# Moving TensorE's branch hint in two mixture-of-experts loops from the head of a pass to a point ahead of its last down projections

## The chip, the cores and the metric

The kernel runs on one core of one Trainium2 chip. The metric is the device time of one execution in microseconds (us), taken as the median of several runs.

## The reference

Two transformer blocks one after the other, batch 1, 256 tokens, width 1024, all in float32. The first block is attention beside a state-space mixer, then a mixture of experts with 16 experts (512 hidden units each, two per token). The second block is three kinds of attention, merged by gates, then a mixture of experts with 32 experts (1024 hidden units each, four per token). What matters here are the two mixtures, cut to their core:

```
for e in range(MOE_EXPERTS):                      # first block, 16 experts
    he = jax.nn.silu(h @ w_gate[e]) * (h @ w_up[e])
    out = out + combine[..., e:e + 1] * (he @ w_down[e])

def expert_block(rows, e):                        # second block, 32 experts
    hb = xt[rows] @ w1[e] + b1[e]
    g, u = clip(hb[:, :D_EXPERT]), clip(hb[:, D_EXPERT:])
    glu = g * jax.nn.sigmoid(g * SWIGLU_ALPHA)
    return ((u + 1.0) * glu) @ w2[e] + b2[e]
```

## The kernel before

Each engine has its own hand-written instruction stream: SyncE (SP) issues the weight loads, TensorE (PE) multiplies, ScalarE (ACT) and VectorE (DVE) do what lies between. They meet at semaphores alone.

**Weights** stream from HBM through a ring of six slots in SBUF (`ring`), 2 MB a load. SP issues the load of a slot when PE has counted the product that read it last (`PD`, "products_done"). An expert of the first mixture reads three slots (gate, up, down), one of the second six (gate and up of the first 512 hidden units, gate and up of the other 512, two down halves).

**The tokens of an expert** are gathered by a matmul with a 0/1 matrix (`gather`, L1676), so an expert multiplies only with the tokens that chose it. Their number comes in three sizes: up to 64, up to 128, and all 256 tokens. `size_of` loads the size of an expert from SBUF into a register, and `by_size` (L376) writes a body once for each size, each inside an `If` on that register. So the compiled program holds three bodies at each such place and runs one. With up to 64 tokens the two halves of the columns run on different halves of the array.

**An expert on PE** (`expert`, L1721) issues in this order:

- `half_up` (L1605, matmuls at L1621, the bias of the second mixture at L1626): the gate half into PSUM pair 0, then the up half into pair 1. The second mixture does both twice.
- between them `scatter` (L1682, matmuls at L1694): the finished rows of the expert before go back to their tokens.
- `turn_hidden` (L1632, L1639): transposes of the hidden rows. In the second mixture it stands twice, and the second one waits for the second half of the hidden units.
- `gather` (L1666, L1676): the rows of the next expert.
- a wait for `outputs_added`, then `half_down` (L1644; L1657 for up to 64 tokens, L1660 for more): one down half in the first mixture, two in the second.
- `turn_picks` (L1700; L1707 for up to 64 tokens, L1709 for more): transposes of the 0/1 matrix.

**The loops.** `experts(b, j0, n)` (L1714) runs mixture `b` with `n` experts. After a first `gather` it opens a loop over pairs of experts: `looped(pe, 0, n // 2)` (L1767) gives 8 passes for the first mixture and 16 for the second, and each pass holds two experts (`par` 0 and 1).
**What sets the order** around the change is the order of calls in `expert` alone. The first loop is called at L1774, between `ranks` (L1598) and the transposes of the residual (`transposes("p0", ...)`, L1777). The second is called at L1881 and is PE's last work.

Of the kernel before, what the change touches and what calls it, by code (L numbers as in the profile page):

```python
# [29 lines left out]
def build(nc, a):  # L30
# [11 lines left out]
    with ctx:  # L42
        sems = {}

        def sem(name):
            if name not in sems:
                sems[name] = ctx.enter_context(nc.semaphore(name))
            return sems[name]
# [247 lines left out]
        def uses_before(j):  # L296

            return 16 * (j // RING + 1)
# [69 lines left out]
        def size_of(eng, e):  # L368

            return eng.value_load(sizes[0:1, bass.ds(e + 1, 1)], min_val=0, max_val=2)  # L370

        def looped(eng, start, end):  # L372

            return nc.Fori(start, end, engines=[eng.engine], hint_back_edge=True)

        def by_size(eng, size, body):  # L376

            for c, w in enumerate((H2, P, T)):
                with eng.If(size == c):
                    body(w)  # L380
# [995 lines left out]
        def _(pe):  # L1376
# [255 lines left out]
            def turn_hidden(b, half, size):  # L1632

                o = ps[2 - b]
                src = HID[:, half]

                def body(w):
                    for c in range(4 * w // P):
                        ins = nc.tensor.transpose(o[:, P * c:P * c + P], src[:, P * c:P * c + P], ident)  # L1639
                    ins.then_inc(sem(f"hidden_turned{b}"), 1)  # L1640

                by_size(pe, size, body)
# [39 lines left out]
            def scatter(b, e, size):  # L1682

                pe.wait_ge(sem(f"ys_ready{b}"), e + 1)

                def body(w):
                    if w == T:
                        pe.drain().then_inc(sem(f"scattered{b}"), 1)
                        return
                    for t in range(NT):  # L1690
                        for h in range(2):
                            r = slice(H2 * h, H2 * h + H2) if w == H2 else slice(0, P)
                            y = YS[r, 0:512] if w == H2 else YS[:, 512 * h:512 * h + 512]
                            ins = mm(ps[2 + t][:, 512 * h:512 * h + 512], pickT[r, P * t:P * t + P], y, start=True,  # L1694
                                     stop=True)
                    ins.then_inc(sem(f"scattered{b}"), 1)

                by_size(pe, size, body)

            def turn_picks(b, buf, size):  # L1700

                def body(w):
                    for t in range(NT):
                        o = ps[1][:, P * t:P * t + P]
                        if w == H2:
                            for h in range(2):
                                ins = mm(o[H2 * h:H2 * h + H2, :], pick[:, buf, t, 0:H2], ident, start=True, stop=True)  # L1707
                        else:
                            ins = nc.tensor.transpose(o, pick[:, buf, t], ident)  # L1709
                    ins.then_inc(sem(f"pick_turned{b}"), 1)  # L1710

                by_size(pe, size, body)

            def experts(b, j0, n):  # L1714

                nh = b
                nk = 3 * nh
                hidden = sem(f"hidden_ready{b}")
                hiddenT = sem(f"hiddenT_ready{b}")

                def expert(i, par, size, size_before, size_next):  # L1721
                    e = 2 * i + par
                    j = j0 + nk * par

                    def value(jj):
                        return 16 * (2 * nk // RING) * i + uses_before(jj)

                    if b == 2:
                        pe.wait_ge(sem(f"b1_loaded{par}"), 16 * i + 16)
                    for half in range(nh):  # L1730
                        if half:
                            pe.wait_ge(sem("gate_limited"), 2 * e + 1)
                        else:
                            pe.wait_ge(sem(f"xg_ready{b}"), e + 1)
                        half_up(j, value(j), ps[0], size, (half, par) if b == 2 else None)
                        if half:
                            pe.wait_ge(up_free, 2 * e + 1)
                        else:
                            pe.wait_ge(sem(f"pickT_ready{b}"), e + 1)
                        half_up(j + 1, value(j + 1), ps[1], size, (2 + half, par) if b == 2 else None)  # L1740
                        j += 2
                        if half == 0:
                            scatter(b, e, size_before)
                    if b == 1:
                        pe.wait_ge(hidden, e + 1)
                        turn_hidden(b, 0, size)
                        gather(b, e + 1, 1 - par, size_next)
                    else:
                        pe.wait_ge(hidden, 2 * e + 1)
                        pe.wait_ge(sem("gate_limited"), 2 * e + 2)  # L1750
                        turn_hidden(b, 0, size)
                        pe.wait_ge(up_free, 2 * e + 2)
                        gather(b, e + 1, 1 - par, size_next)
                        pe.wait_ge(hidden, 2 * e + 2)
                        pe.wait_ge(hiddenT, 2 * e + 1)
                        turn_hidden(b, 1, size)
                    pe.wait_ge(sem(f"outputs_added{b}"), e + 1)
                    for half in range(nh):
                        pe.wait_ge(hiddenT, nh * e + (half + 1))
                        half_down(j, value(j), HIDT[:, half], size, half == 0, half == nh - 1)  # L1760
                        j += 1
                    if b == 2:
                        pe.wait_ge(sem(f"xg_ready{b}"), e + 2)
                    turn_picks(b, par, size)

                gather(b, 0, 0, size_of(pe, 0))
                with looped(pe, 0, n // 2) as i:  # L1767
                    for par in range(2):
                        e = 2 * i + par
                        expert(i, par, size_of(pe, e), size_of(pe, e - 1), size_of(pe, e + 1))  # L1770
                pe.wait_ge(sem(f"pickT_ready{b}"), n + 1)
                scatter(b, n, size_of(pe, n - 1))  # L1772

            experts(1, n_front1, n1_exp)  # L1774
            J = {k: base_mid + n for k, n in after1.items()}
            pe.wait_ge(sem("moe1_added"), 1)
# [102 lines left out]
            pe.wait_ge(sem("acc_ready"), 1)  # L1879
            all_free("cb")  # L1880
            experts(2, base_exp2, NE2)  # L1881

# [24 lines left out]
```

## Time and profile before

| what | value |
|---|---|
| median of 3 runs | 2607.18 us |
| lowest and highest run | 2602.42, 2622.62 us |
| the profiled execution's own time | 2602.19 us |
| its span, first to last instruction | 2600.3 us |
| mean granted TensorE clock | 0.907 of full speed |

The rows below come from that one profiled execution. Its times are microseconds from the start of the span. In the timeline a row is: start, duration, engine, line, operation, tiles written and read, count of instructions merged into the row, and in brackets the idle time ahead of them with what ended it. "issue" there means that nothing which the profile shows held the engine back. The first mixture's loop lies between about 478 and 754 us, the second's between 1372 and 2573 us.

### The profile page before, as it was taken

The page shows a single profiled execution, that of the slowest core. Times are in us where ns is not written, and L with a number is a line of the kernel's source. Part 1 is how long each engine was busy: PE and PEld are TensorE (multiplying, and loading weights), DVE is VectorE, ACT ScalarE, POOL GpSimd, SP SyncE. Part 2 cuts the span into 40 slices and gives each one's busy share as a digit, 9 for nine tenths or more (in the row PEclk, how much of TensorE's full clock was granted, in tenths as well). Part 3 has the DMA queues.
Part 4 walks back from the last instruction along what each step waited for, and adds up shares of the span by engine and source line. Part 5 has one row for each costly group of instructions (what it writes and reads, how often), then busy time and mean ns, then how long its engine had stood idle before and what let it go on. Part 6 is the DMA issues. An engine that isn't in the chain of part 4 may idle for free.

```text
span 2600.3 us, 32457 instructions
## 1 busy us (share of the span) xinstructions
PE 2267.8 (87%) x12228; PEld 1336.9 (51%) x12229; DVE 589.6 (23%) x1216; ACT 365.5 (14%) x714; POOL 6.5 (0%) x23
## 2 busy tenths in 40 slices
PE   7966787899988997788858999999989999999996
PEld 5655344566644686533335554544544555555443
DVE  3354212122214014500022111121211112222112
ACT  1021101121111013400011110101011111111111
POOL 0000000000000000000000000000000000000000
PEclk9976897899999986688878999999999999999998
DMA  8820242599975331022226997869799999999980
GB/s 293 294 96 0 97 173 86 203 367 363 362 269 192 132 140 55 1 95 99 97 75 239 367 370 292 293 245 352 283 352 358 364 386 372 359 365 366 360 326 17
DMA packets 272729, 621.11 MB, mean 239 GB/s; under 512 B 12200, under 2 KB 19026, under 8 KB 272510
## 3 DMA queue, kind: packets, MB, share of 16 engines
q1 hardware_dynamic: 272302, 616.95, 64.8%
q8 instruction: 207, 3.39, 0.5%
q10 hardware_dynamic: 208, 0.67, 0.1%
q14 instruction: 12, 0.10, 0.0%
HBM read 616.55 MB, written 1.05 MB: 238 GB/s over the span
## 4 chain that ended last, share of the span: by engine, by line
PE 75%; issue 6%; DVE 5%; ACT 2%; ACTq 0%; DVEq 0%
PE pair L1621 25%; PE pair L1414 12%; PE pair L1657 10%; PE pair L1676 8%; PE pair L1694 4%; PE pair L1626 3%; PE pair L1401 3%; PE pair L1660 2%; PE pair L1463 1%; PE pair L1829 1%; PE pair L1426 1%; PE pair L1455 1%; PE pair L1438 1%; PE pair L1707 1%; PE pair L1418 1%
## 5 line engine op out<-in xcount | busy, mean ns | idle before, releaser
L1621 PE MATMUL pair<-ring,r_at 128*64 128x256 f32 (+1 forms) x4864 | 669.8, 407 | 83.1 <-issue 79.4
L1621 PEld LDWEIGHTS pair<-ring,r_at 128*64 128x64 f32 (+1 forms) x4864 | 387.5, 145 | 355.3 <-issue 220.6
L1657 PE MATMUL pair<-ring,r_big 128*64 128x512 f32 x1152 | 256.9, 596 | 0.4 <-issue 0.4
L1414 PE MATMUL pair<-ring,x_T 128*128 128x512 f32 (+1 forms) x608 | 236.9, 545 | 2.9 <-ACT r_big L721 1.5
L1676 PE MATMUL pair<-r_big,r_mix 128*128 128x64 f32 (+1 forms) x1600 | 199.1, 285 | 20.7 <-DVE r_big L1342 10.0
L1676 PEld LDWEIGHTS pair<-r_big,r_mix 128*128 128x128 f32 x1600 | 192.4, 200 | 32.4 <-issue 31.5
L1177 DVE TENSOR_SCALAR r_big<-iota,rank 128x128 f32<-128x128 f32 x100 | 24.1, 284 | 780.6 <-PE pair L1626 624.7
L1414 PEld LDWEIGHTS pair<-ring,x_T 128*128 128x128 f32 x608 | 107.5, 190 | 127.0 <-issue 124.9
L1401 PE MATMUL pair<-x_T,ring 128*128 128x256 f32 x656 | 152.7, 391 | 8.0 <-DVEq L840 6.6
L1657 PEld LDWEIGHTS pair<-ring,r_big 128*64 128x64 f32 x1152 | 79.0, 137 | 145.4 <-issue 144.3
L1401 PEld LDWEIGHTS pair<-x_T,ring 128*128 128x128 f32 x656 | 125.7, 195 | 32.5 <-issue 8.0
L1694 PE MATMUL pair<-r_at,r_big 64*128 64x512 f32 (+1 forms) x400 | 110.1, 626 | 9.5 <-issue 8.2
L1192 DVE SCALAR_TENSOR_TENSOR r_big<-pair,combine,r_big 128x512 f32<-128x512 f32 x132 | 90.0, 744 | 51.1 <-PE pair L1694 50.6
L815 ACT ACTIVATE r_big<-r_big 128x256 f32<-128x256 f32 (+1 forms) x64 | 28.4, 444 | 506.3 <-DVE r_big L1340 506.3
L1414 PE MATMUL pair<-ring,r_big 128*128 128x512 f32 x144 | 78.5, 706 | 22.6 <-DVE r_big L1073 6.8
L1414 PE MATMUL pair<-ring,r_at 128*128 128x512 f32 x192 | 92.2, 644 | 3.8 <-issue 2.4
L1626 PE MATMUL pair<-r_big,ones 1*64 1x256 f32 (+1 forms) x480 | 90.4, 416 | 0.0
L1342 DVE TENSOR_SCALAR r_big<-pair 128x256 f32<-128x256 f32 (+1 forms) x64 | 29.3, 458 | 230.4 <-PE pair L1626 230.4
L1694 PEld LDWEIGHTS pair<-r_at,r_big 64*128 64x128 f32 (+1 forms) x400 | 39.0, 189 | 59.2 <-issue 59.2
L697 ACT COPY r_at<-pair 128x512 f32<-128x512 f32 (+1 forms) x48 | 29.8, 622 | 278.3 <-PE pair L1657 223.8
L1414 PEld LDWEIGHTS pair<-ring,r_at 128*128 128x128 f32 x192 | 39.7, 209 | 54.3 <-issue 54.3
L1414 PEld LDWEIGHTS pair<-ring,r_big 128*128 128x128 f32 x144 | 32.0, 228 | 67.0 <-issue 54.5
(306 smaller groups left out, 1577.7 us busy)
## 6 DMA issues: line engine op xcount, KB each, us to landing
ring<-exp_w SPq DMA_DIRECT2D x192, 2048.0 KB, 11.0
ring<-w_in SPq DMA_DIRECT2D x24, 2048.0 KB, 8.1
ring<-w_gate SPq DMA_DIRECT2D x16, 2048.0 KB, 10.4
ring<-w_up SPq DMA_DIRECT2D x16, 2048.0 KB, 12.4
ring<-w_down SPq DMA_DIRECT2D x16, 2048.0 KB, 8.2
ring<-mod_w SPq DMA_DIRECT2D x12, 2048.0 KB, 13.4
ring<-w_out SPq DMA_DIRECT2D x4, 2048.0 KB, 9.8
ring<-w_branch SPq DMA_DIRECT2D x3, 2048.0 KB, 7.7
```

Source lines behind the costliest of these rows:

```text
L697: s.copy(YS[:, 0:n], ps[2][:, 0:n]).then_inc(sem(f"ys_ready{b}"), 1)
L815: s.activation(SG[:, 0:4 * w], GS[:, 0:4 * w], ACT.Sigmoid, scale=1.702)\
L1192: ins = v.scalar_tensor_tensor(out=dst[:, t, 512 * h:512 * h + 512], in0=ps[2 + t][:, 512 * h:512 * h + 512], scalar=comb0[:, t, bass.ds(e ...
L1342: v.tensor_scalar(US[:, c], ps[1][:, c], 7.0, -7.0, ALU.min, ALU.max).then_inc(up_free, 1)
L1401: ins = mm(out[:, ct], w[:, k, c0 + P * ct:c0 + P * ct + P], xT[:, k], start=(k == 0), stop=(k == nk - 1 and bias is None))
L1414: ins = mm(out[:, t, 0:n], xT[:, k, P * t:P * t + P], w[:, k, c0:c0 + n], start=(k == 0), stop=(k == nk - 1 and bias is None))
L1621: ins = mm(out, stat(k), w_[:, k, c0:c0 + n], start=(k == 0), stop=(bias is None and k == KD - 1))
L1626: ins = mm(out, ones[32 * q:32 * q + 1, 0:rows], b1q[32 * q:32 * q + 1, buf, c0:c0 + n], start=False, stop=True)
L1657: ins = mm(ps[2][H2 * h:H2 * h + H2, 0:512], hT[:, at:at + H2], cols, start=beg, stop=end)
L1660: ins = mm(ps[2 + t][:, 512 * h:512 * h + 512], hT[:, 512 * t + P * f:512 * t + P * f + P], cols, start=beg, stop=end)
L1676: ins = mm(ps[b - 1][:, P * k:P * k + w], HT[:, t, P * k:P * k + P], pick[:, buf, t, 0:w], start=(t == 0), stop=(t == NT - 1))
L1694: ins = mm(ps[2 + t][:, 512 * h:512 * h + 512], pickT[r, P * t:P * t + P], y, start=True, stop=True)
```

## The change

The hint is taken from the head of a pass. The PE loops are now written out by hand in place of the helper: a counter register, the branch to the head, the add and the compare-and-branch. The hint is marked inside the second expert of each pass (`par` 1), behind the transposes of the hidden rows and ahead of the wait for `outputs_added` and of the down halves. Both mixtures' loops are changed, on PE alone.

```diff
@@ expert(i, par, size, size_before, size_next)
                         pe.wait_ge(hidden, 2 * e + 2)
                         pe.wait_ge(hiddenT, 2 * e + 1)
                         turn_hidden(b, 1, size)
+                    at = pe.mark_branch_hint_location() if par else None
                     pe.wait_ge(sem(f"outputs_added{b}"), e + 1)
                     for half in range(nh):
                         pe.wait_ge(hiddenT, nh * e + (half + 1))
...
                     turn_picks(b, par, size)
+                    return at
 
                 gather(b, 0, 0, size_of(pe, 0))
-                with looped(pe, 0, n // 2) as i:
+                count = nc.alloc_registers(f"pair_of_experts{b}", engines=[pe.engine])
+                head, tail = f"experts{b}_head", f"experts{b}_tail"
+                nc.regs_mov(count, 0)
+                nc.br(head, engines=[pe.engine])
+                with nc.body(head, valid_engines=[pe.engine]):
+                    i = nc.snap(count, min_val=0, max_val=n // 2 - 1)
                     for par in range(2):
                         e = 2 * i + par
-                        expert(i, par, size_of(pe, e), size_of(pe, e - 1), size_of(pe, e + 1))
+                        at = expert(i, par, size_of(pe, e), size_of(pe, e - 1), size_of(pe, e + 1))
+                    nc.regs_alu(count, count, 1, op=mybir.AluOpType.add)
+                    pe.br_lt(count, n // 2, on_true=head, on_false=tail).branch_hint(at)
+                nc.switch_bb(tail)
```

## Rows read from the trace of the kernel before

**Rows 1.** The page: engines, the chain's shares, and the queues of DMA

```profile
PE 2267.8 (87%) x12228; PEld 1336.9 (51%) x12229; DVE 589.6 (23%) x1216; ACT 365.5 (14%) x714; POOL 6.5 (0%) x23
...
q8 instruction: 207, 3.39, 0.5%
...
PE 75%; issue 6%; DVE 5%; ACT 2%; ACTq 0%; DVEq 0%
```

**Rows 2.** Waits of PE, 1365 to 2590 us: total, times, longest us

```profile
PE pair L1621 <- issue: 74.9, 16, 6.4
```

**Rows 3.** Timeline of PE over one pass of the second loop and its back edge

```profile
2021.52 0.65 PE L1626 MATMUL pair<-r_big,ones 1*64 1x256 f32 x4
...
2033.65 0.61 PE L1707 MATMUL pair<-ident,r_big 128*64 128x128 f32 x8
2034.21 3.67 PE L1621 MATMUL pair<-ring,r_at 128*64 128x256 f32 x32
...
2048.67 3.67 PE L1621 MATMUL pair<-ring,r_at 128*64 128x256 f32 x32
...
2057.49 7.09 PE L1657 MATMUL pair<-ring,r_big 128*64 128x512 f32 x32
2064.41 0.61 PE L1707 MATMUL pair<-ident,r_big 128*64 128x128 f32 x8
2070.90 5.53 PE L1621 MATMUL pair<-ring,r_at 128*64 128x256 f32 x32 [5.88 <-issue]
```

**Rows 4.** Windows around that edge: us, five engines' busy, clock, DMA share, GB/s

```profile
2061.00:2065.00 4.00, 4.00 (x26) 1.49 (x22) 0.00 (x0) 0.37 (x1) 0.00 (x0) 1.00 1.06 391
2065.00:2071.00 6.00, 0.12 (x4) 0.12 (x4) 0.00 (x0) 1.77 (x3) 0.00 (x0) 0.74 1.03 405
2071.00:2076.00 5.00, 5.00 (x30) 3.07 (x32) 0.00 (x0) 0.00 (x0) 0.00 (x0) 0.63 0.88 347
```

**Rows 5.** Timeline of PE at the three back edges that differ

```profile
1682.58 7.12 PE L1621 MATMUL pair<-ring,r_at 128*128 128x512 f32 x16 [2.28 <-issue]
...
1774.50 5.25 PE L1621 MATMUL pair<-ring,r_at 128*64 128x256 f32 x32 [2.67 <-issue]
...
1846.81 13.90 PE L1660 MATMUL pair<-ring,r_big 128*128 128x512 f32 x32
1860.55 0.38 PE L1709 MATMUL pair<-ident,r_big 128*128 128x128 f32 x2
1860.86 3.67 PE L1621 MATMUL pair<-ring,r_at 128*64 128x256 f32 x32
```

**Rows 6.** DMA by window: a pass (1994.2:2065), 2065:2066.6, 2066.6:2070.9, 1853:1855

```profile
DMA packets 10510, 25.50 MB, mean 360 GB/s; under 512 B 202, under 2 KB 202, under 8 KB 10499
...
q8 instruction: 11, 0.18, 1.0%
...
q8 instruction: 1, 0.02, 4.3%
...
q1 hardware_dynamic: 443, 1.76, 102.8%
...
q8 instruction: 1, 0.02, 3.0%
```

**Rows 7.** DMA by window: 500:755 (this queue alone), and 755:761

```profile
q1 hardware_dynamic: 39750, 92.48, 100.9%
...
q8 instruction: 1, 0.02, 1.2%
```

**Rows 8.** Timeline of PE at the end of the first loop

```profile
743.16 1.99 PE L1694 MATMUL pair<-r_at,r_big 64*128 64x512 f32 x8
...
754.51 0.68 PE L1694 MATMUL pair<-r_at,r_big 64*128 64x512 f32 x1 [1.30 <-ACT r_big L699]
760.92 3.49 PE L1694 MATMUL pair<-r_at,r_big 64*128 64x512 f32 x7 [5.73 <-issue]
```

**Rows 9.** DMA by window, 2559:2574, the last pass: all packets in it

```profile
DMA packets 1, 0.02 MB, mean 1 GB/s; under 512 B 0, under 2 KB 0, under 8 KB 0
q8 instruction: 1, 0.02, 0.4%
```

## Prediction, made before the changed kernel was run

> **What bounds the kernel now.** I read the page first. TensorE (PE) is busy 87% of the span and the chain that ended last is 75% PE [rows 1]. The list of who waited for whom, taken over the second expert loop (1365 to 2590 us), has one large entry: L1621, the first up half of an expert, 74.9 us in 16 waits put down to "issue", the longest 6.4 [rows 2]. "Issue" means that no semaphore is to blame: the instructions themselves were late.
>
> [...]
>
> **What the old hint does.** Four rows tell. (a) Entering the block behind the first loop finds it missing, though it is the next in line: ahead of the branch something else had been chosen for loading, and for a loop that is resident that costs no packet. (b) A taken back edge of the second loop has one packet before PE restarts [rows 6], so it is the head; the block behind the loop isn't fetched too. (c) With the middle size the packet lies in 1853 to 1855 us, PE being busy until 1860.86 [rows 5, 6]. (d) In the last pass, where the branch is not taken, a packet comes too, between 2559 and 2574 [rows 9]. I read: the hint, though 2,550 instructions old, works, and the head is requested when the sequencer enters the block that holds the branch. It comes late because only 97 instructions lie between, most of them skipped. Where the data queues are full (share 1.03 in 2065 to 2071 [rows 4]) the head isn't there in time; where the down halves take 13.90 us in place of 7.09 [rows 3, 5] it is.
>
> [...]
>
> **The change, part by part.**
> Loop control (a register set, an add, a compare-and-branch in place of the helper's): the same instructions; 0.
> The hint leaves the head: one instruction fewer before the first L1621. In the gap of 5.88 us this is hidden by the fetch; where there is no fetch, by the picks, which run without a gap into L1621 (2034.21 [rows 3]). It comes back in the second expert, behind the turned hidden half, where the sequencer is ahead of 7 us of down halves; 0. Bounds: nothing and 15 x 0.1 us.
> No DMA, no wait and no semaphore moves; SP's, ACT's and DVE's loops keep their hint at the head.
>
> Second loop: the new hint stands some 293 instructions ahead of the branch, so 60 behind one boundary and 196 ahead of the last. If the request is made on entering the branch's block, nothing changes: the hint was in force at that moment before and is now. Term: 0. Bounds: all of rows 2's 74.9 us with its clock loss gone, or one more fetch on each edge (both below).
>
> First loop: the hint stands 162 instructions ahead of the branch, so behind the last boundary (248 ahead). On entering that block no hint is in force, and the next in line, the block behind the loop, is loaded, once, in the first pass. Hint and branch then find the head resident, as now. The exit finds its code: the 5.73 us go. The seven scatter matmuls took 3.49 us there against 1.99 for eight in a pass [rows 8], which may give 1.5 us more; I leave that as a bound. What is late next: nothing of the fetch, the next block being asked for 5.7 us sooner too. Bounds of this term: 0 to 7.2; taken: 5.7, the gap itself, since the chain through scatter, the addition on DVE and L1426 has no other source at work there.
>
> Sum: 2602.2 (profiled run; span 2600.3) - 5.7 - 0 = 2596.5 us. The median of the three runs is 2607.2 with 2602.4 to 2622.6, so a median a few us above the sum is as likely; I say 2597.
>
> **Rivals.**
> 1. *The hint asks for its block at once.* Then the old one was wasted on a block that was just being executed, and the new one asks 7 us before the branch, with the head not in the engine. For: a late hint is what such a mechanism wants, and no row shows a hint executed while its target was away. Against: the packet of the old kernel, (a) to (d), is then hard to place. Price if the head is always in time: 74.9 us of gaps plus about 2 us of slow clock on 12 edges (1.86 in rows 3), 99 us. But DMA then bounds: a pass moves 25.5 MB, at 390 GB/s [rows 4, 6] 65.4 us, against 69.3 - 7.8 = 61.5 us of PE. The ring gives credit: a slot freed at 2022.2 is read again at 2048.67, 26.5 us later [rows 3], and its load takes 11 to 12, so 14 us may be used up. Eight short passes in a row need 8 x 3.9 = 31 us, so 17 come back as waits on ring slots. 2602 - 99 + 17 - 6 = 2514 us.
> 2. *At once, but behind the sequential fetch.* The block of the branch is being asked for at the same time. Its packet and the head's stand some 6 us apart now; if the second request waits for the first, the head comes about 2 to 3 us sooner: 12 edges x 2.7, with 1 us of clock each, 44 us: 2602 - 44 - 6 = 2552 us. DMA isn't reached.
> 3. *Slower: the choice is made before the hint.* If what follows the branch's block is settled on entering the block before it, 60 instructions ahead of the new hint, the second loop loads the block behind itself first and the head only on demand. Place: the gap at L1621; price: one more fetch, 3.6 to 6 us by the closest packets of a pass, 12 x 4.3 = 52 us, and the first loop still gains: 2602 + 52 - 6 = 2648 us. It decides as soon as a pass shows 12 packets instead of 11. Against: a choice made so early would have helped the old kernel hide the head, and it didn't.
> [...]
>
> **How the numbers follow.** Forecast 0.46; rival 1: 0.17; rival 2: 0.16; rival 3: 0.11; rival 4: 0.10. A measurement of this kernel tells about 1% from no change, 26 us. Rivals 1 and 2 are faster by more than that: 0.33. Forecast and rival 4 are within: 0.56. Rival 3: 0.11. Range: the forecast's own is 2588 to 2612 (bounds of the exit term, spread of the runs). To leave out no more than 2 in 10 it must take in rivals 1 and 2, down to 2505, and leaves out rival 3.
>
> **What would show it.** Right: L1694 after the first loop runs as x8 without its 5.73 us; the waits of L1621 on issue over the second loop stay at 70 to 78 us; 11 packets a pass; the packet beside the picks stays where it is, and the queue's total of 207 stays within 2. [...] Waits of L1621 on DMA into the ring late in the second loop would show rival 1 reaching the DMA bound.

## The result, and the profile after

The changed kernel is slower. Its median is 2637.25 us (six runs, 2630.38 to 2641.41), that of the kernel before on the same chip 2612.99 us (six runs, 2602.42 to 2622.62). The ratio is 1.0092, with a 95% interval of 1.0062 to 1.0121. The prediction was 2597 us, with a range from 2505 to 2612.

| | before | after |
|---|---|---|
| profiled execution, us | 2602.19 | 2630.38 |
| span, us | 2600.3 | 2628.6 |
| mean granted TensorE clock | 0.907 | 0.895 |
| first to last L1621 of the second loop, us | 1171.4 | 1206.5 |

The page after, the lines of [rows 1]:

```profile
PE 2276.6 (87%) x12228; PEld 1342.4 (51%) x12229; DVE 589.6 (22%) x1216; ACT 365.3 (14%) x714; POOL 6.5 (0%) x23
...
q8 instruction: 221, 3.62, 0.6%
...
PE 74%; issue 7%; DVE 5%; ACT 2%; ACTq 0%; DVEq 0%
```

There are as many matmuls as before, and 14 more packets of code. The waits of PE, 1365 to 2625 us, answer to [rows 2]:

```profile
PE pair L1621 <- issue: 101.8, 15, 8.4
```

That is 26.9 us more of idle time at one place. The timeline of PE, at the end of the first loop ([rows 8] of before), at three edges that [rows 5] shows, and at an edge of the common kind ([rows 3]):

```profile
757.87 1.99 PE L1694 MATMUL pair<-r_at,r_big 64*128 64x512 f32 x8 [1.29 <-ACT r_big L699]
762.73 3.57 PE L1426 MATMUL pair<-ident,x_resid 128*128 128x128 f32 x16 [2.88 <-DVEq L840]
...
1689.25 9.72 PE L1621 MATMUL pair<-ring,r_at 128*128 128x512 f32 x16 [7.08 <-issue]
1789.47 5.63 PE L1621 MATMUL pair<-ring,r_at 128*64 128x256 f32 x32 [8.38 <-issue]
1876.53 3.67 PE L1621 MATMUL pair<-ring,r_at 128*64 128x256 f32 x32 [0.40 <-issue]
...
2073.74 7.09 PE L1657 MATMUL pair<-ring,r_big 128*64 128x512 f32 x32
2080.66 0.61 PE L1707 MATMUL pair<-ident,r_big 128*64 128x128 f32 x8
2088.62 6.24 PE L1621 MATMUL pair<-ring,r_at 128*64 128x256 f32 x32 [7.35 <-issue]
```

In the timeline a gap stands in brackets. Three things are to be seen. The scatter behind the first loop is one row of eight matmuls without the 5.73 us stall, as forecast. The common edges now stand idle for 6.5 to 7.6 us each, this one for 7.35, where the one of before was 5.88. And the edges that had lost little, 2.28, 2.67 and nothing, now show 7.08, 8.38 and 0.40.

The DMA by window says what the gap is made of: 2015 to 2089 us (a pass with its edge), then 2080 to 2083 and 2083 to 2088.6 us (the gap itself, in two parts). Before, a pass had 11 instruction packets, one of them at the edge [rows 6].

```profile
q8 instruction: 12, 0.20, 1.1%
...
q8 instruction: 2, 0.03, 5.7%
...
q1 hardware_dynamic: 563, 2.25, 100.9%
```

Two packets now lie at the edge, 1.15 us apart (they begin at 2081.56 and 2082.71), and then none until PE starts again at 2088.62, 5.9 us after the second one began. Before, the one packet of the edge began at 2065.35, and PE started 5.55 us later. The windows of the gap and of what follows (2082 to 2088.6, and 2088.6 to 2094.8), beside [rows 4]:

```profile
2082.00:2088.60 6.60, 0.00 (x0) 0.00 (x0) 0.00 (x0) 1.28 (x1) 0.00 (x0) 0.62 1.02 401
2088.60:2094.80 6.20, 6.18 (x34) 3.54 (x34) 0.00 (x0) 0.00 (x0) 0.00 (x0) 0.58 0.56 221
```

The granted clock behind the longer gap is 0.58 over 6.2 us, where it was 0.63 over 5 us ([rows 4], and 1.00 ahead of the gap): the first up half takes 6.24 us and not 5.53. The prediction's 5.9 + 1.9 us of a back edge are the gap of 5.88 and the 5.53 us that stand in [rows 3] for the 3.67 inside a pass.

**The sum.** Second loop: 12 common edges with 7.16 us of gap each (101.8 less the three others, over 12) where they had 5.8, so about 16; the three others 4.8, 5.7 and 0.4, 10.9; and the slow clock behind the gaps, 8 to 9 (0.7 us at the edge shown; over the program the busy time of L1621 rises from 669.8 to 678.9 us). Together 35 to 36, where the loop's length shows 35.1 (1206.5 - 1171.4). From the first up half of the first loop to that of the second the program takes 10.3 us less (899.3 for 909.6). Of these, 7.2 are the stall of 5.73 and 1.5 of slow clock, and 2.1 are the passes themselves, 34.35 us each for 34.62, with the hint gone from their head. The spans differ by 28.3 us and not by 35.1 - 10.3, because the profiled execution also took 5.5 us more ahead of the first loop, in code that is the same, and 2.0 less behind the second. The medians differ by 24.3.

**What the changed program holds.** The profile counts the instructions that were executed. The first line of the page, before and after, and between them what the trace of before has on PE at the line of the helper's loop (L1767), with the shortest, median and longest ns of one and the first and last start:

```profile
span 2600.3 us, 32457 instructions
...
L1767 PEldq BRANCH_PREFETCH_HINT  x24: 36/40/55, 466.8 to 2484.0; - x24
L1767 PEldq FUSED_REGOPS  x24: 68/68/68, 467.0 to 2484.1; - x24
L1767 PEldq ALU_OP  x24: 36/36/36, 508.2 to 2566.7; - x24
L1767 PEldq COMPARE_BRANCH  x24: 85/3499/5197, 508.3 to 2566.8; - x24
L1767 PEldq MOVE  x2: 34/36/37, 466.7 to 1376.1; - x2
...
span 2628.6 us, 32433 instructions
```

Before, PE executes one hint in each of the 8 + 16 passes, as an instruction of its own (the first at 466.8 us, 0.1 behind the register move ahead of the loop), and one compare-and-branch at the end of each pass, which lasts up to 5.2 us. The changed kernel executes 24 instructions fewer, and its trace has no BRANCH_PREFETCH_HINT on PE at all. The instructions of PE's compiled stream around the second loop's head, before:

```
L1767 UNCONDITIONAL_BRANCH
L1767 BRANCH_PREFETCH_HINT
L1767 ISA
L370 TENSOR_LOAD sizes
```

and after:

```
L1772 UNCONDITIONAL_BRANCH
L1774 ISA
L370 TENSOR_LOAD sizes
```

Between the hidden transposes and the down halves, where the source marks it, there is no BRANCH_PREFETCH_HINT either, in neither loop. The change did not move the hint, it took it out. In the source the mark is the first thing behind the last `If` of `turn_hidden` and is followed by a wait; nothing of PE's own stands ahead of it in that block. Put one register move ahead of it (run 2 below) and the hint appears, at the intended place. At which step between the source and the compiled stream it is lost was not looked into.

### The profile page after: what moved, and what is told of

The parts are those of the page before. It is cut to its first block, busy times and chain, and to the rows that moved or that the text cites. A ratio compares the mean times of both kernels' runs of the same rounds, so it can differ in the third digit from the quotient of the medians.

```text
span 2628.6 us, 32433 instructions
## 1 busy us (share of the span) xinstructions
PE 2276.6 (87%) x12228; PEld 1342.4 (51%) x12229; DVE 589.6 (22%) x1216; ACT 365.3 (14%) x714; POOL 6.5 (0%) x23
## 3 DMA queue, kind: packets, MB, share of 16 engines
HBM read 616.55 MB, written 1.05 MB: 235 GB/s over the span
## 4 chain that ended last, share of the span: by engine, by line
PE 74%; issue 7%; DVE 5%; ACT 2%; ACTq 0%; DVEq 0%
PE pair L1621 25%; PE pair L1414 12%; PE pair L1657 10%; PE pair L1676 8%; PE pair L1694 4%; PE pair L1626 3%; PE pair L1401 3%; PE pair L1660 2%; PE pair L1463 1%; PE pair L1839 1%; PE pair L1426 1%; PE pair L1707 1%; PE pair L1455 1%; PE pair L1418 1%; PE pair L1438 1%
## 5 line engine op out<-in xcount | busy, mean ns | idle before, releaser
L1621 PE MATMUL pair<-ring,r_at 128*64 128x256 f32 (+1 forms) x4864 | 678.9, 411 | 109.1 <-issue 105.1
L1621 PEld LDWEIGHTS pair<-ring,r_at 128*64 128x64 f32 (+1 forms) x4864 | 390.3, 147 | 387.3 <-issue 253.5
L1657 PE MATMUL pair<-ring,r_big 128*64 128x512 f32 x1152 | 256.9, 596 | 0.0
L1657 PEld LDWEIGHTS pair<-ring,r_big 128*64 128x64 f32 x1152 | 78.9, 137 | 145.0 <-issue 143.9
L815 ACT ACTIVATE r_big<-r_big 128x256 f32<-128x256 f32 (+1 forms) x64 | 28.3, 443 | 542.2 <-DVE r_big L1340 542.2
L1463 PE MATMUL pair<-r_big,r_at 128*128 128x64 f32 (+2 forms) x272 | 50.9, 357 | 20.4 <-ACT r_at L609 20.4
L1414 PEld LDWEIGHTS pair<-ring,r_big 128*128 128x128 f32 x144 | 32.3, 230 | 67.2 <-issue 54.8
```

What stands on the lines that cost most here:

```text
L1414: ins = mm(out[:, t, 0:n], xT[:, k, P * t:P * t + P], w[:, k, c0:c0 + n], start=(k == 0), stop=(k == nk - 1 and bias is None))
L1463: ins = mm(ps[3][:, 512 * (c % 2) + w * h:512 * (c % 2) + w * h + w], PT[0:rows, c % 2, h * nt + kt], map_values(kind, 4 * hc + h, kt), st ...
L1621: ins = mm(out, stat(k), w_[:, k, c0:c0 + n], start=(k == 0), stop=(bias is None and k == KD - 1))
L1657: ins = mm(ps[2][H2 * h:H2 * h + H2, 0:512], hT[:, at:at + H2], cols, start=beg, stop=end)
```

## The experiments

The theory at this point (T): without a hint, the sequencer entering the block that holds the branch asks for the block behind the loop, and for the head only when the branch is taken, one request later. With a hint in force at that entry it asks for the head. The rivals are these: the old hint at the head was good and a late one is bad (R1: its place matters), a late hint asks for its block at once (R2, rivals 1 and 2 of the prediction), and the hand-written loop in itself costs something (R3).

The runs stand in one table, in order; medians in us, the ratio with its 95% interval to the kernel before on the same chip. Issue is PE's wait of the first up half on issue over the second loop; the last column is the count of instruction packets.

| run | what | median (runs) | ratio | issue | packets |
|---|---|---|---|---|---|
| 1 | no hint | 2642.05 (4) | 1.0114 [1.006, 1.0167] | 100.7 | 221 |
| 2 | late hint, really there | 2595.06 (10) | 0.9951 [0.9918, 0.9983] | 68.2 | 207 |
| 3 | hint at head, second loop only | 2599.86 (10) | 0.995 [0.9918, 0.9982] | 77.3 | 207 |
| 4 | hint 29 instructions ahead | 2643.75 (4) | 1.0116 [1.006, 1.0172] | 101.4 | 222 |
| 5 | hint 458 ahead | 2600.65 (1) | | 73.3 | 207 |
| 6 | run 2, aligned | 2556.47 (4) | 0.9791 [0.9738, 0.9844] | 32.3 | 193 |
| 7 | run 2, bodies in other order | 2595.86 (1) | | 36.0 | 207 |
| 8 | runs 6 and 7 together | 2579.81 (4) | 0.9883 [0.9833, 0.9934] | 12.6 | 193 |
| 9 | hints at head, aligned | 2576.38 (4) | 0.9877 [0.9835, 0.9919] | 33.8 | 193 |
| 10 | no hint, aligned | 2640.33 (1) | | 96.2 | 207 |
| 11 | run 2, half of the weights loaded | 2516.3 (1) | | 24.6 | 207 |

The kernel before had medians of 2610.34 (19 runs) beside runs 1 to 4, 2613.69 (7) beside 5 to 8 and 2609.94 (7) beside 9 to 11.

### Run 1: the hand-written loop, no hint in the source

```diff
+                    pe.br_lt(count, n // 2, on_true=head, on_false=tail)
```

(the loop as in the change, without the mark and without `branch_hint`)

> The changed kernel with the hint taken out of the source altogether, in both loops. Theory A (the changed kernel's compiled program has lost the hint, and all of its loss is the missing hint): same as the changed kernel, median 2632 to 2642 us, waits of L1621 on issue over the second loop 98 to 106 us, 221 instruction packets, no gap at the exit of the first loop. Theory B (the hint is there but comes after the choice of what to load next, my rival 3): also near the changed kernel if a late hint is ignored, but not the same packet count if the late hint does anything at all.

Measured: 2642.05 us, 221 packets, the exit of the first loop without its stall. The waits of PE over the second loop:

```profile
PE pair L1621 <- issue: 100.7, 15, 7.9
```

It is the changed kernel again, within the spread of the runs. So what the change did to the time is what leaving the hint out does.

### Run 2: the late hint, kept

```diff
+                spare = nc.alloc_registers(f"spare{b}", engines=[pe.engine])
+                def mark():
+                    nc.regs_mov(spare, 0)
+                    return pe.mark_branch_hint_location()
...
-                    at = pe.mark_branch_hint_location() if par else None
+                    at = mark() if par else None
```

> The change as it was meant: an unused register move ahead of the mark, so that the hint stands in the compiled program of both loops, 293 and 162 instructions ahead of the branches. Theory A: the time comes back to that of before or better. If the request is made on entering the branch's block (my forecast): 2602 - 6 = 2597 to 2607 us, gaps of 5.9 us, 207 packets, no exit gap. If the hint asks at once: gaps below 4 us, 2515 to 2560 us. Theory B: 2632 to 2642 us and gaps of 7.2 us as in the changed kernel.

Measured: 2595.06 us, span 2592.9. The trace has 24 hints on PE again. They are shown with PE's waits on issue at L1621 over the second loop, the scatter behind the first loop, and an edge of each kind:

```profile
L1725 PEldq BRANCH_PREFETCH_HINT  x24: 36/45/55, 506.6 to 2549.6; - x24
...
PE pair L1621 <- issue: 68.2, 16, 5.8
...
754.25 1.99 PE L1694 MATMUL pair<-r_at,r_big 64*128 64x512 f32 x8 [1.30 <-ACT r_big L699]
...
1449.28 5.09 PE L1621 MATMUL pair<-ring,r_at 128*64 128x256 f32 x32 [5.70 <-issue]
...
1773.98 3.67 PE L1621 MATMUL pair<-ring,r_at 128*64 128x256 f32 x32 [2.00 <-issue]
```

This is the kernel that the prediction was about: the exit's 5.73 us are gone, the second loop keeps its gaps and its 207 packets, and the median is 2 us from the 2597 forecast. That nearness is partly luck: the forecast lay 5.7 us under a base of 2602, and run 2 lies 15 us under its own base of 2610 (interval 4 to 21). R1 and R3 fall: the same loop with a late hint is as fast as with an early one, a little faster than before. R2 falls for this place of the hint: the trace has the hint executed at 2049.69, 6.0 us ahead of the branch, and the head's packet begins only at 2058.02, behind that of the last block (2052.02) and 6.0 us after it, as in the kernel before.

### Run 3: the hint at the head of the second loop, none in the first

```diff
+                    at = pe.mark_branch_hint_location() if b == 2 else None
```

> Hand-written loops, hint at the head of the second loop only, none in the first. Both theories: second loop as before (L1621 on issue 75 us, 11 packets a pass), the first loop's exit gap of 5.73 us gone as in the changed kernel: 2595 to 2607 us, 5 to 7 us under the kernel before. If hand-written loop control cost something, it would show here as a time above before's.

Measured: 2599.86 us, the same ratio as run 2; 77.3 us of issue, the exit stall of the first loop gone. The first loop, in which no run has an instruction packet between 514 us and its last closing branch at 749 us or later, needs no hint, and one at its head costs the exit (5.73 us in before [rows 8], 5.75 in run 9). The second loop needs one, at its head or late (77.3 and 68.2 us of issue, 100.7 without).

### Runs 4 and 5: the place of the hint in the second loop

```diff
@@ run 4: behind the down halves
+                    at = None
                     if b == 2:
+                        at = mark() if par else None
                         pe.wait_ge(sem(f"xg_ready{b}"), e + 2)
@@ run 5: ahead of the gather of the second expert
                         turn_hidden(b, 0, size)
+                        at = mark() if par else None
                         pe.wait_ge(up_free, 2 * e + 2)
```

> Second loop only: the hint ahead of the picks, 29 instructions ahead of the branch and behind the last block boundary (93 ahead); none in the first loop. If the request is made only on entering the branch's block, the hint is too late and this is the changed kernel: 2632 to 2642 us, 12 packets a pass. If the hint asks at once, the head's packet comes a little sooner than on demand, because the sequencer is some 16 matmuls ahead: gaps of 6 to 7 us, 2620 to 2635 us.

> Second loop only: the hint 458 instructions ahead of the branch, ahead of the last two block boundaries (349 and 93 ahead). Theory A (request for the head on entering the branch's block, whatever the hint's age): gaps of L1621 as with the hint at the head or 293 ahead, 68 to 77 us in sum over the second loop, 207 packets. Theory B (a hint asks at once if its block is away): the head comes 7 us or more ahead of need, gaps below 2 us, sum under 20 us, and 15 packets may be added.

By the count of compiled instructions the last block boundary of the second loop is 93 ahead of the branch. Run 4's hint stands 29 ahead, behind that boundary; run 5's 458 ahead, as far as two boundaries before it. Waits of PE over the second loop, run 4 and run 5:

```profile
PE pair L1621 <- issue: 101.4, 14, 7.6
```

```profile
PE pair L1621 <- issue: 73.3, 16, 6.1
```

Run 4 is as slow as the kernel without a hint (2643.75 us); run 5 is as fast as those with one (2600.65, one run). Between 2548 instructions ahead (run 3) and 293 (run 2) the place makes no difference that these runs tell (68 to 77 us of waits, 74.9 before), and between 293 and 29 it decides the time. What is fetched next is thus settled between 293 and 29 instructions ahead of the branch; the boundary at 93 lies there, and no other. That the moment is the entry into the block, and not a fixed distance from the branch, is what run 6 tests by moving the boundary.

The hint of run 4 isn't ignored, though. DMA from 2605 to 2620 us, behind the last pass, in run 4 and then in run 1:

```profile
q8 instruction: 2, 0.03, 1.0%
...
q8 instruction: 1, 0.02, 0.6%
```

Run 4 fetches one block more there (222 packets for 221), 0.7 us behind its last hint (2610.74, the hint at 2610.07), though the branch isn't taken. The sequencer is ahead of PE by about what the expectation says: at the common edges of run 4 the closing branch begins with 12 to 14 of PE's matmuls still to start, and in run 1 with 12 to 16. At the common edges its head's packet begins 3.0 us after the branch is executed, where runs without a hint have 3.7. So a hint behind the boundary does ask at once, as R2 says. It gains nothing: the other block was asked for already, the head's packet takes 2.0 us beside it (1.7 in run 1, 1.1 with a hint in force), and PE starts 4.3 us after its end, as at the edges of the other runs.

### Run 6: the loop aligned, so that the last boundary lies far ahead of the branch

```diff
                 nc.regs_mov(count, 0)
+                if b == 2:
+                    pe.addr_align(256, offset=0, max_nops=0)
                 nc.br(head, engines=[pe.engine])
```

(over run 2)

> The late hint kept as in e2, and the second loop's head put on a block boundary, so that its last boundary moves from 94 to 244 instructions ahead of the branch, behind the first down half's code instead of the second's. Nothing else moves. Theory A: the head is asked for 16 matmuls (3.5 us) sooner, gaps fall from 5.5 to 2 to 3 us, sum 68 to some 30 to 35 us, the slow clock after them shrinks too: 2535 to 2560 us, 10 packets a pass instead of 11. Theory B (the wait is the fetch itself, in line behind the block's own fetch, and not the moment of the request): 2590 to 2600 us, gaps of 5 us.

The head now begins a block of 256, so a pass of some 2,550 is ten blocks where it was eleven with a rest at each end (the DMA view below has ten packets for the 2,548 instructions that run 3 has from its hint at the head to the branch, 255 each), and its last boundary is 244 ahead of the branch. Measured: 2556.47 us, 2.1% under the kernel before (interval 1.6 to 2.6), and the best of the runs that load all weights. Waits of PE over the second loop, and the edge:

```profile
PE pair L1621 <- issue: 32.3, 27, 2.3
PE pair L1694 <- issue: 5.5, 1, 5.5
```

```profile
2102.54 7.09 PE L1657 MATMUL pair<-ring,r_big 128*64 128x512 f32 x32
2109.46 0.61 PE L1707 MATMUL pair<-ident,r_big 128*64 128x128 f32 x8
2112.30 5.36 PE L1621 MATMUL pair<-ring,r_at 128*64 128x256 f32 x32 [2.24 <-issue]
```

The head's packet begins at 2106.91, inside the last down half. PE restarts 5.4 us later, as in run 2, but 3.2 of these are now covered by work. Eleven edges are of this kind (2.0 to 2.4 us), three show 0.8 us. There the head's packet ended 4.9 us or more before PE starts, so about 0.8 us of an edge is left even where the code is in time. DMA by window, 2046 to 2112.3, one pass:

```profile
DMA packets 10609, 25.97 MB, mean 392 GB/s; under 512 B 200, under 2 KB 200, under 8 KB 10599
...
q8 instruction: 10, 0.16, 1.0%
```

From L1621 to L1621 at the edges, seven passes take 461.7 us (1979.26 to 2440.97), 66.0 each; five of before take 69.5 each (2000.59 to 2348.23), six of after 71.5 (2017.61 to 2446.42). There is a price: the exit of the second loop, whose code lay in the last block before, is now its own block, 5.5 us once where it was 2.4.

### Runs 7 and 8: the body that runs put last in its block

Each `by_size` compiles the body for 64 tokens first. In these runs `half_down` writes it last (the order 2, 1, 0), so that the instructions that are skipped lie ahead of the executed ones and the boundary is passed sooner. Run 7 is over run 2, run 8 over run 6. The kernels are one line longer at that place, so L1621 is L1622 there, and L1657 is L1658.

```diff
-        def by_size(eng, size, body):
+        def by_size(eng, size, body, order=(0, 1, 2)):
-            for c, w in enumerate((H2, P, T)):
+            for c in order:
+                w = (H2, P, T)[c]
...
-                by_size(pe, size, body)
+                by_size(pe, size, body, (2, 1, 0))
```

> As e2, but the down halves' three bodies stand in the order 256, 128, 64 tokens, so that the one that mostly runs is the last; the boundary stays 94 instructions ahead of the branch but is now crossed ahead of the second down half's matmuls instead of behind them. Theory A: gaps of 2 to 3 us, sum 30 to 40 us, 2535 to 2565 us, still 11 packets. Theory B: as e2, sum near 68 us.

> Both: boundary 244 ahead of the branch and bodies swapped, so the branch's block is entered ahead of both down halves, 7 us before the branch. Theory A: gaps below 1 us, sum under 10 us, clock 1.00 through the passes; PE then needs 61 to 62 us a pass and the ring's loads become the bound late in the loop (65 us a pass), waits of L1621 on DMA appear: 2500 to 2525 us. Theory B: no better than e6.

Both missed. Run 7 measured 2595.86 (one run) where a gain was expected. Its waits of PE over the second loop:

```profile
PE pair L1622 <- issue: 36.0, 14, 4.2
PE pair L1658 <- issue: 21.1, 26, 1.3
```

The edges lost 32 us of their 68, and 21 came back inside the pass, at the down halves. Run 8 measured 2579.81, where run 6 had 2556.47:

```profile
PE pair L1658 <- issue: 25.6, 20, 1.5
PE pair L1622 <- issue: 12.6, 16, 1.2
```

and at the edge of a pass 0.8 us is left (0.8 to 1.2 at 14 edges, none at one), with another gap ahead of the down halves:

```profile
2047.48 7.09 PE L1658 MATMUL pair<-ring,r_big 128*64 128x512 f32 x32 [1.38 <-issue]
2054.39 0.62 PE L1708 MATMUL pair<-ident,r_big 128*64 128x128 f32 x8
2055.82 3.67 PE L1622 MATMUL pair<-ring,r_at 128*64 128x256 f32 x32 [0.82 <-issue]
```

The theory about the edge holds (under 1 us at 13 of 15 edges where the boundary comes early, as expected) and the theory about the time does not: the idle time was moved, not removed. PE's issue waits come to 38 us in these two rows as against 32 in run 6, and the pass is no shorter, 66.7 us for 66.0 (seven passes, 1990.39 to 2457.56). Code packets of run 8 begin 5.9 to 8 us apart (2032.14, 2038.46, 2044.46, 2050.41, 2056.37 and so on), ten in a pass. The data queue is busy all of the time too (share 1.02, 380 GB/s from 2000 to 2400 us), and whether the code or the data sets the 66 us was not told apart; no wait of PE for a ring slot shows, so it is at least not a late weight load. Run 8's span is 17.4 us over run 6's. Of these, 8 stand in the second loop and 9.6 ahead of it (its first up half begins at 1385.8 and 1376.2). The swapped bodies account for 3 of the 9.6: the first loop, where they are swapped too, takes 272.3 us from its first up half to its last in run 8, 271.9 in run 7 and 269 in runs 2 and 6. Four more lie ahead of the first loop, in code that is the same in all kernels, and differ by as much between executions (the first loop begins between 471.9 and 478.0 us in the profiles here).

### Runs 9 and 10: the hint at the head, and none, in the aligned loop

```diff
@@ run 9, over the loop of run 6
+                    at = pe.mark_branch_hint_location()
                     i = nc.snap(count, min_val=0, max_val=n // 2 - 1)
@@ run 10
-                    pe.br_lt(count, n // 2, on_true=head, on_false=tail).branch_hint(at)
+                    pe.br_lt(count, n // 2, on_true=head, on_false=tail)
```

> Both hints at the head as in the kernel before, in hand-written loops, and the second loop's head on a block boundary as in e6. Theory A (where the hint stands doesn't matter to the second loop, the block boundary does): second loop as e6, gaps of 2.2 us, 193 packets; the first loop's exit gap of 5.7 us is back: 2555 to 2570 us. Theory B (late hint and alignment both count): second loop worse than e6 by 10 us or more, 2570 us and over.

> No hint in either loop, the second loop's head on a block boundary. Theory A: the block behind the loop is asked for on entering the last block and the head only at the branch: gaps of 6 to 7.5 us, alignment gives the edge almost nothing, 11 packets a pass (one less than 12): 2620 to 2640 us.

Waits of PE over the second loop, run 9, then run 10:

```profile
PE pair L1621 <- issue: 33.8, 27, 2.4
PE pair L1694 <- issue: 5.7, 1, 5.7
```

```profile
PE pair L1621 <- issue: 96.2, 26, 6.9
```

Run 9's edges are those of run 6 in gaps and packets, whatever the age of the hint. By its time the expectation was missed: 2576.38 us lies above the 2555 to 2570 of theory A, and in what theory B gave for the time (2570 and over). Its first loop has the stall again, in the timeline:

```profile
757.05 0.68 PE L1694 MATMUL pair<-r_at,r_big 64*128 64x512 f32 x1 [1.30 <-ACT r_big L699]
763.49 3.49 PE L1694 MATMUL pair<-r_at,r_big 64*128 64x512 f32 x7 [5.75 <-issue]
```

With the slow clock behind it that is 7.2 of the 18.2 us between the spans of runs 9 and 6. Two more are the first loop's passes, 34.64 us each with the hint at the head for 34.40. Some 9 stand in the length of the second loop (1138.4 against 1129.4 us), with gaps that are only 1.5 longer in sum; the two ran on different chips, and what these 9 are was not settled, so that a late hint is worth something of its own in the aligned loop is not excluded. Run 10 gives 2640.33 (one run), where run 1 had 2642.05: alignment without a hint is worth nothing here. The packets show why. Without a hint the head's begins 3.6 to 3.7 us after the branch is executed (medians of the common edges), in run 10 as in the changed kernel and run 1, wherever the boundary lies. With a hint it begins 2.3 us after the branch in the kernel before and in run 2, and 0.6 us ahead of it in run 6: there it goes by the boundary.

### Run 11: half of the data

```diff
-                sp.dma_start(dst, src.rearrange("(t p) n -> p t n", p=P)).then_inc(slot_loaded[slot], 16)
+                src = src.rearrange("(t p) n -> p t n", p=P)
+                sp.dma_start(dst[:, 0:nk // 2], src[:, 0:nk // 2]).then_inc(slot_loaded[slot], 16)
```

(over run 2; lines one higher; the kernel leaves out half of each weight load and so does not compute the mixture, it serves for the time alone)

> As e2, but the second loop's weight loads bring only the first half of each slot (half of the bytes; the rest of a slot keeps what it held, so this leaves out half of the weights); the queue is idle half of the time. [...] If the fetch has a fixed length: gaps as in e2, sum 68 us.

Measured: 2516.3 us (one run). The window from 2000 to 2400 us, the waits of PE over the second loop, and one edge:

```profile
2000.00:2400.00 400.00, 386.21 (x2886) 216.84 (x2886) 85.02 (x179) 53.31 (x100) 0.00 (x0) 1.00 0.60 202
```

```profile
PE pair L1622 <- issue: 24.6, 14, 2.4
```

```profile
2085.32 0.61 PE L1708 MATMUL pair<-ident,r_big 128*64 128x128 f32 x8
2087.82 3.67 PE L1622 MATMUL pair<-ring,r_at 128*64 128x256 f32 x32 [1.90 <-issue]
```

It is the same code with the same place of the boundary and the same 207 packets, and the common edges are 1.5 to 2.4 us in place of 5.3 to 5.8 (one 1.9), at a DMA share of 0.60. The packet of the head begins 3.7 us after the one ahead of it (2078.57, 2082.26); in run 2, with full queues, it is 6.0 (2052.02, 2058.02). The DMA share of these stretches is 0.02 (2078.6 to 2082.3) and 1.05 (2050.5 to 2058). In the median over the edges that wait, the head's packet begins 1.2 us ahead of the branch here and 2.3 us behind it in run 2. From the begin of the head's packet to PE's restart it is 5.2 to 5.9 us here and 5.4 to 5.8 there. So what the weight stream delays is the begin of the code packet. The gap of an edge is that delay and the 5.2 to 5.9 us behind it, less what PE still has to do when the block is asked for. A fetch of fixed length, whatever the queues carry, is ruled out: it would have left the 68 us of run 2 where 24.6 stand.

## Why the prediction was wrong

**The step that failed** is that of the second loop: "the new hint stands some 293 instructions ahead of the branch ... nothing changes: the hint was in force at that moment before and is now". Its place was right: compiled with a spare instruction ahead, the hint does stand 293 ahead. But in the changed kernel no hint was in force in any pass, because the compiled program holds none. I took a line of the source for an instruction of the engine. The term was forecast at 0 and measured +35.1 us (27 of gaps, 8 of clock).

**The rule behind it stood.** "The head is requested when the sequencer enters the block that holds the branch": runs 2, 3 and 5 (hint ahead of the last boundary: 207 packets, 68 to 77 us) and run 4 (behind it: 222 packets, 101 us) show it, and run 6 shows that the distance from boundary to branch sizes the gap. The forecast had that distance at 97 instructions; in the compiled stream of before it is 94. The sizes it was counted with stand too: one gate or up half (L1621) with up to 64 tokens is 16 calls in the source and 32 matmuls in [rows 3], the page has as many weight loads (12,229) as matmuls (12,228), and run 6 has 255 instructions to a packet, for the 256 taken. What the old hint was worth could have been worked out ahead of the runs too: with it the loop asks once at the edge, without it twice.

**The exit of the first loop**: forecast -5.7, bounds 0 to 7.2. Gone in every kernel without a hint in that loop's head, and in run 2; with the slow clock behind it 7.2 us, the upper bound. It came about in the changed kernel for a second reason beside the one given: not that the hint stood behind the boundary, but that there was none. Both leave the block behind the loop as the next to load.

**The hint leaves the head** was put at 0, with 1.5 us as a bound for the second loop's 15 edges and none for the first loop. A pass of the first loop takes 34.62 us with the hint at its head (34.64 in run 9) and 34.35 to 34.46 in every kernel without, 2.1 us over eight passes. At the second loop's edges PE starts 5.5 us after the begin of the head's packet in the kernel before and in run 3, and 5.4 in runs 2 and 5, so 0.1 us an edge, as the bound had it.

**Rival 3** (slower, 2648 us, chance 0.11) had the right signs: 12 packets a pass, the head on demand, the first loop's gain kept. Its reason was a choice made too early, and run 2 speaks against it: a hint 57 instructions behind the boundary at 350 and ahead of the one at 94 works in full. Its price was too high. I took one more fetch at 4.3 us, since I thought of two fetches one behind the other. The two requests overlap: their packets begin 1.15 us apart at the edge shown, and a common edge lost 1.4 us. It was dearer only at the edges where the hint had been nearly in time (4.8 and 5.7 us), which I had not priced.

**Rivals 1 and 2** (a hint that asks at once, 2514 and 2552): run 2 has gaps of 5.3 to 5.8 us at 11 of the 12 common edges (1.9 at one), where they would give none, or 3 to 4, and in run 5 two packets lie between the hint (2055.3) and the head's packet (2068.8). They fell for a hint ahead of the last boundary. Behind it, in run 4, the hint does ask at once, too late to gain. That run 6 reaches 2556 is not rival 2: in run 9 the hint is 2,548 instructions old and the gap is the same.

**Rival 4** (no effect, 2602, chance 0.10) was not tested by the changed kernel, which has no hint; it fell with run 2, where the late hint stands and the exit's 5.73 us are gone. Without a hint (after and run 1) there are 221 packets, two at an edge, of which I take the first for the block behind the loop, as no view names a packet's content, and the common edges of run 1 stand idle for 6.4 to 7.7 us. With a hint ahead of the last boundary there are 207, and the head's begins 2.3 us after the branch (before and run 2).

The range was wrong on its upper side for want of one case: that the edit does not do what it says. Rival 4 held "no effect" but not "the hint is lost", though a loss could be priced from [rows 5 and 6]: at least one more packet on each of 15 edges, and the two cheap edges at full price.

## What to carry to other kernels

When an edit is about a marker, a hint or an attribute, look for it in the compiled instructions before anything is read into a time; a mark that stands alone behind an `If` can vanish without a word. By these runs a long loop that fetches its code anew in each pass (11 packets a pass here) needs a branch hint in force before the last block boundary ahead of its closing branch, no matter how old it is (68 to 77 us of waits with a hint 293 to 2,548 instructions old, 101 without), and then its cost is set by how much work lies between that boundary and the branch: keeping the hint late gave 0.5% here (with the gain at the first loop's exit in it), and with the head of the loop aligned as well it was 2.1% (2556 us). The first loop, which has no code packet from its second pass to its exit, was better without one at its head: the hint there cost its exit 7.2 us once, and 0.3 us in each pass.

## What the hardware showed that was not expected

- Two requests for code made in a row overlap: 1.0 to 1.9 us between the begins of their packets at the changed kernel's common edges. In run 4 the second begins 0.8 us after the first and takes 2.0 us in place of 1.1.
- From the end of the head's packet to PE's first matmul it is 4.1 to 4.9 us at the edges where PE waits for it (medians 4.2 to 4.4 in before, after and runs 1 to 6), with full data queues and with a DMA share of 0.60 (run 11, 4.2 to 4.7). The packet itself takes about 1.1 us ahead of that; where the 4.2 go no view shows.
- A hint executed behind the last boundary makes a request of its own (run 4: one packet more behind the last pass, and the head's packet 3.0 us after the branch for 3.7).
- What full data queues add is ahead of the packet. The last two packets of a pass begin 3.7 us apart in run 11 at the edge shown, some 6.0 in run 2 and before (2059.39, 2065.35). Elsewhere in a pass of before, with queues as full (share 1.04 from 2025 to 2039 us), single pairs are as close as 3.9 us (2028.32, 2032.18); why these are not delayed stays open.
- Ten blocks at that spacing are 60 of a pass's 66 us. In run 8 the gaps went from the edge into the body, and PE waited 25.6 us at the down halves: asking for code earlier stopped paying there. Fewer instructions in a pass would be the next thing to try, and was not tried.
